# Attention pairs: rounded-half projections, modulation rows as VectorE dot products, turned values, and a softmax shared by two engines

## What is computed

```python
mod_x = silu(c) @ w_ada + b_ada            # 6 x 1024 values: shifts, scales, gates
ux = (rms_norm(x, norm1) * (1 + sc1) + sh1) @ w_in
uc = (rms_norm(xc, norm1) * (1 + csc1) + csh1) @ w_in
fx, qx, kx, vx, bx, cx, hx = split_in(ux)  # Fourier, q, k, v, conv parts
attn_x = na_latent(qx * scale, kx, vx, kc, vc, rpb)   # 8 heads of 64
x = x + g1 * mix_out(fx, attn_x, conv_x, w_fourier, w_out)
...                                        # then a hierarchical MoE of 32 experts,
...                                        # and four layers: sb, moba, swa, sb
```

## Time and profile before

| | |
|---|---|
| median of 3 runs | 2013.89 us (2011.30 to 2018.54) |
| profiled execution, its own time | 2015.65 us |
| its span | 2013.8 us, mean TensorE clock 0.972 |
| PE / PE weight loads / DVE / ACT / POOL busy | 1813.1 / 1450.8 / 1112.1 / 755.4 / 72.8 us |
| chain that ended last | PE 65%, DMA 24%, DVE 7%, ACT 2% |
| HBM read | 549.63 MB |

### The profile page before, as it was taken

How to read it: one execution, slowest core, us unless ns; L and a number is a source line. 1 busy time by engine, 2 the same in 40 slices (tenths; PEclk the granted TensorE clock), 3 DMA queues, 4 the chain that set the end, 5 groups by cost and what they waited for, 6 DMA issues and landing times.

```text
span 2013.8 us, 33860 instructions
## 1 busy us (share of the span) xinstructions
PE 1813.1 (90%) x14214; PEld 1450.8 (72%) x14214; DVE 1112.1 (55%) x1876; ACT 755.4 (38%) x1270; POOL 72.8 (4%) x131
## 2 busy tenths in 40 slices
PE   7999976776776789999999899999999999999998
PEld 5788744443443479788888688887688888988887
DVE  0233311101110278788677888764778877777774
ACT  2121200000000247644545654444554445755443
POOL 0200000000000000100000000000010000000000
PEclk8999999889899899999999999999999999999999
DMA  9457799999999975864773574466284578334533
GB/s 405 199 222 315 309 429 427 429 428 430 428 428 429 426 310 205 337 230 167 295 305 146 210 287 173 167 279 276 105 342 181 182 277 318 135 114 168 192 142 127
DMA packets 42186, 552.40 MB, mean 274 GB/s; under 512 B 6496, under 2 KB 6880, under 8 KB 7008
## 3 DMA queue, kind: packets, MB, share of 16 engines
q1 hardware_dynamic: 33408, 454.22, 56.7%
q0 software_dynamic: 8672, 96.67, 11.5%
HBM read 549.63 MB, written 1.05 MB: 273 GB/s over the span
## 4 chain that ended last, share of the span: by engine, by line
PE 65%; DMA 24%; DVE 7%; ACT 2%; issue 1%; SPq 0%; DVEq 0%; ACTq 0%
PE bank L594 24%; PE bank L595 12%; DMA ada_ring<-in_moe_side 12%; PE bank L589 10%; DMA ring<-in_moe 7%; PE bank L574 4%; PE bank L655 2%; DMA ring<-in_down 2%; PE bank L583 2%; PE bank L872 2%; PE bank L631 1%; DMA ring<-in_v 1%; DMA ring<-in_mix 1%; PE bank L1159 1%; PE bank L1027 1%
## 5 line engine op out<-in xcount | busy, mean ns | idle before, releaser
L595 PE MATMUL bank<-acts,ring_parts 128*128 128x256 f32 x2248 | 631.6, 281 | 0.0
L595 PEld LDWEIGHTS bank<-acts,ring_parts 128*128 128x128 f32 x2248 | 426.5, 190 | 0.0
L594 PE MATMUL bank<-acts,mixT_parts 128*128 128x512 f32 x1096 | 391.0, 399 | 6.3 <-DVE ring_parts L2395 6.0
L594 PE MATMUL bank<-acts,xn_parts 128*128 128x512 f32 x736 | 259.9, 396 | 0.0
L594 PEld LDWEIGHTS bank<-acts,mixT_parts 128*128 128x128 f32 x1096 | 207.1, 189 | 58.7 <-DVE ring_parts L2395 5.9
L1308 ACT CAST mixT_parts<-ring 128x1024 fp32r<-128x1024 f32 (+1 forms) x152 | 152.4, 1004 | 204.8 <-PE bank L595 184.9
L2059 DVE TENSOR_TENSOR mixT<-mixT,bank 128x128 f32<-128x128 f32 x32 | 9.2, 288 | 340.1 <-ACT mixT L1449 340.1
L594 PEld LDWEIGHTS bank<-acts,xn_parts 128*128 128x128 f32 x736 | 138.1, 188 | 32.9
L1308 ACT CAST xn_parts<-ring 128x1024 fp32r<-128x1024 f32 x96 | 100.2, 1052 | 141.2 <-PE bank L595 139.9
L589 PE MATMUL bank<-acts,ring_parts 128*128 128x256 f32 x504 | 141.7, 281 | 0.0
L2397 DVE TENSOR_TENSOR ring_parts<-ring,mixT_parts 128x1024 fp32r<-128x1024 f32 x88 | 107.7, 1225 | 30.0 <-ACT mixT_parts L1308 30.0
(11 more groups left out here) (326 smaller groups left out, 3166.4 us busy)
## 6 DMA issues: line engine op xcount, KB each, us to landing
ring<-in_moe SPq DMA_DIRECT2D x48, 2048.0 KB, 27.2
ada_ring<-in_moe_side SPq DMA_DIRECT2D x48, 2048.0 KB, 25.9
ada_ring<-in_ada POOLq DMA_DIRECT2D x45, 2048.0 KB, 13.4
ring<-in_gu SPq DMA_DIRECT2D x44, 2048.0 KB, 7.8
ring<-in_down SPq DMA_DIRECT2D x32, 1408.0 KB, 6.4
ring<-in_na SPq DMA_DIRECT2D x12, 2048.0 KB, 10.8
ring<-in_qk SPq DMA_DIRECT2D x12, 2048.0 KB, 9.4
ring<-in_out SPq DMA_DIRECT2D x10, 2048.0 KB, 9.0
```

The lines of the kernel that those rows point to most:

```text
L594: mm(dst[:, :], w[0], both(*x), start=start, stop=False)
L595: return mm(dst[:, 0:T], w[1], x[0], start=False, stop=stop)
```

## The change

- q, k, v weights of a pair come as three DMAs of 0.5 MB (`na_w`) into thirds of one slot; the two modulation chunks of a pair are laid out anew, one output column per partition.
- All projections of the pairs become `split_product`: `hT` and `hcT` are cut into halves once (`x_parts` in `xsq` and `hT`, `ctx_parts` in `ada_ring1`), and each third of the weights per pair (`cast_pair` on ACT, `low_pair` on DVE). v is projected like q and k (256 tokens moving), copied by ACT to `vt` and turned by four transposes on PE.
- The modulation rows are no longer PE's: DVE takes, per pair, eight dot products of 1024 elements per partition (`ada_dots`, `tensor_tensor_reduce`) against `c_row`, silu(c) repeated on all partitions, which PE makes once at the start from `c_spread` (two products of 512 columns, one DVE product ahead).
- Scores are laid out latent / context by bank; DVE scales and biases the latent half in two instructions of 128x512, ACT the context half; ACT also normalises (`ACT.Copy` with a scale per row) and copies all four banks of turned probabilities.
- The first pair's q, k and context k projections are placed between the steps of the Fourier section. The loops over pairs are unrolled.
- First sb layer: ACT's `group_out` moves from round j = 0 to round j = 1, behind the cast of `sp_hi`; PE's wait for it moves behind the scores of j = 1.

```diff
@@ SP @@
+                elif name == "na":
+                    for j in range(NA_PAIRS):
+                        def pair_weights(x, landed_in):
+                            if x == 2 or j == 0:
+                                wait_used(sp, n0 + 3 * j - RING)
+                            else:
+                                sp.wait_ge(na["qk_proj"] if x else na["q_used"], j)
+                            sp.dma_start(w_pair[x], ins["na_w"][3 * j + x]).then_inc(landed_in, 16)
...
+                        pair_weights(0, na["q_landed"])
+                        pair_weights(1, na["k_landed"])
+                        pair_mods(0)
+                        pair_weights(2, landed[n0 % RING])
+                        pair_mods(1)
@@ PE @@
+            def pair_project(dst, x, j, tokens, ready=None):
+                pe.wait_ge(attn_lo, 3 * j + x + 1)
+                lo = w_pair_lo[x].rearrange("p (k n) -> p k n", k=KT)
+                for k in range(KT):
...
+                    m = split_product(dst, (w_pair_hi[x][:, k, :], lo[:, k, :]), tuple(t[:, k, :] for t in tokens), k == 0, k == KT - 1)
+                return m
...
                 if not last:
-                    pe.wait_ge(na["qk_ready"], j + 1)
-                    ada(n0 + 1, bank[2][:, 0:T], r)
-                    ada(n0 + 2, bank[0][:, 0:T], r)
+                    pair_project(bank[1][:, T:2 * T], 2, j, ctx_parts).then_inc(used[n0 % RING], 1)
...
                 if not last:
-                    pe.wait_ge(na["ada_row"], j + 1)
-                    ada_columns(bank[2][:, 0:4], ada_rows[:, 0, :], 1)
-                    ada_columns(bank[2][:, 4:8], ada_rows[:, 1, :], 1).then_inc(na["ada_done"], 1)
+                    pe.wait_ge(na["vt_ready"], j + 1)
+                    for t in range(4):
+                        m = nc.tensor.transpose(bank[1][:, t * P:(t + 1) * P], vt[:, t * P:(t + 1) * P], cst("ident"))
+                    m.then_inc(na["row_done"], 1)
@@ ACT @@
             def na_pair(j, first, last):
+                if not first:
+                    act.wait_ge(na["scores"], j)
+                    for h in range(2):
+                        m = A(soft[:, 2 * h:2 * h + 2, T:2 * T], bank[6 + h][:, :].rearrange("p (q n) -> p q n", q=2), ACT.Copy, scale=SCALE)
+                    m.then_inc(na["s_ready"], 1)
+                if not first and not last:
+                    cast_pair(j, 2)
...
+                    act.wait_ge(na["step"], 2 * j)
+                    act.wait_ge(na["e_ready"], j)
+                    for c in range(4):
+                        m = A(prob[:, c, :], prob[:, c, :], ACT.Copy, scale=stat[:, 3, c:c + 1])
+                    m.then_inc(na["p_ready"], 1)
...
+                    wait_used(act, FIRST["na"], j)
+                    copy(vt, bank[1][:, :]).then_inc(na["vt_ready"], 1)
@@ DVE @@
+            def ada_dots(j, q0, q1):
+                for q in range(q0, q1):
...
+                    m = V.tensor_tensor_reduce(w, w, c_row, 1.0, 0.0, ALU.mult, ALU.add, stat[:, 4 + q // 4, q % 4:q % 4 + 1])
+                    if q % 4 == 3:
+                        m.then_inc(used[n % RING], 1)
@@ first sb layer, PE and ACT @@
+                            sb_scores(j)
                             if j == 1:
                                 pe.wait_ge(ada_taken, g + 1)
-                            sb_scores(j)
...
+                        if i == 0 and j == 1:
+                            group_out(group_of(i, 2), "attn")
                         if j < PAIRS - 1:
                             cast_piece(i, V_PIECES + 2 * (j + 1) + 1)
...
-                        if i == 0 and j == 0:
-                            group_out(group_of(i, 2), "attn")
```

More of the change, by code:

```diff
@@ L699, in _ @@
             m.then_inc(ada_cols, 1)
+            pe.wait_ge(na["row_ready"], 1)
+            for c in range(2):
+                m = mm(bank[6 + c][:, :], cst("ones"), c_spread[:, 512 * c:512 * (c + 1)], start=True, stop=True)
+            m.then_inc(na["row_done"], 1)
             n = FIRST["mix"]
             wait_chunk(pe, n)
-            rows(bank[0][:, :].rearrange("p (t n) -> p t n", t=TT), chunk3(n, 512), 0, T, hT, ready=0).then_inc(mix_proj, 1)
+            rows(bank[0][:, :].rearrange("p (t n) -> p t n", t=TT), chunk3(n, 512), 0, T, hT, ready=0).then_inc(mix_pe, 1)
             project(bank[1][:, 0:T], chunk3(n, 512), 256, hT)
@@ L792, in na_pair @@
                                 hp = slice(64 * h, 64 * h + 64)
[L793 removed]
+                                m = mm(bank[4 + 2 * a + h][:, q * T:(q + 1) * T], qk[hp, q * P:(q + 1) * P], keys[hp, :], start=True, stop=True)
                     m.then_inc(na["scores"], 1)
             na_pair(0, True, False)
[L797 removed]
+            for j in range(1, NA_PAIRS):
                 na_pair(j, False, False)
@@ L1420, in _ @@
             na_pair(0, True, False)
-            with act.Fori(1, NA_PAIRS) as j:
+            for j in range(1, NA_PAIRS):
                 na_pair(j, False, False)
@@ L1907, in na_pair @@
                     m.then_inc(na["s_ready"], 1)
-                    dve.wait_ge(na["s_ready"], j)
-                    V.tensor_reduce(stat[:, 0, :], soft[:, :, :], AX.X, ALU.max).then_inc(na["mx"], 1)
+                    dve.wait_ge(na["s_ready"], 2 * j)
+                    V.tensor_reduce(stat[:, 0, :], soft[:, :, :], AX.X, ALU.max).then_inc(na["step"], 1)
                     row_softmax_in(na, j)
+                if not last:
+                    low_pair(j, 2)
+                    ada_dots(j, 0, 2)
@@ L1938, in _ @@
             na_pair(0, True, False)
-            with dve.Fori(1, NA_PAIRS) as j:
+            for j in range(1, NA_PAIRS):
                 na_pair(j, False, False)
```

184 lines of the change are left out of this document (112 added, 72 removed).

## The result

The changed kernel takes **1985.45 us** (median of 4 runs, 1984.24 to 1988.75) against 2015.80 for the kernel before beside it (median of 4): ratio 0.986, 95% interval 0.9835 to 0.9885. It is faster by 1.4%; 1985 was forecast. The forecast took 28.7 us off a base of 2013.89, and the medians here stand 30.4 apart, so that the time itself came out within half a microsecond is partly luck. The profiled execution took 1985.69 us, its span is 1983.8, against 2015.65 and 2013.8.

A forecast was written before the change was run, and what follows sets the result against it. The prediction took PE to bound the pairs, busy 27.80 of 27.80 us. Its terms, -22.6 - 10.2 - 1.5 + 5.9 + 1.7 - 2.0 = -28.7, led from the median 2013.89 to 1985 us, range 1978 to 2007.

The forecast's parts named there:

- Dot products: DVE in the pairs: each 1024-element dot product with its sum costs 1.25 us, plus 0.1 for the read.
- Rival 1: DVE in the pairs: the dot runs at half rate, 2.3 us each, total 2005 us; chance 0.15.
- Rounds: Pairs after the first: 20.85 us, then 20.5 twice, 61.9 where 84.5 were; -22.6 us.
- DVE's loop without waits: DVE in a pair: 20.4 us, as long as PE's; also written 8c + 8.6, c the cost of a dot.
- First pair: From the Fourier section to the first scores: they end at 90.2 us instead of 100.4; -10.2 us.
- the clock term: PE at the start, 32 to 37 us: two products of 512 columns fill an idle stretch; -1.5 us.
- they delay nothing: Start of the kernel: the two 512-column products hold up nothing, since the first `mix` chunk lands behind them.
- out_0: Behind the last scores: output weights land 10.2 us after issue, so PE stands still 5.9 us; +5.9 us.
- clock +1.7: Output products: PE's wait for the output weights slows TensorE's clock after it; +1.7 us.
- sb layer: First sb layer: moving ACT's copy one round later removes PE's wait for q and k of j = 1; -2.0 us.
- Rival 3: Behind the pairs: the output weights are not late, -7.6 us more, total 1977 us; chance 0.09.
- rival 4: Expert stream: paced by transfers that can't start earlier, so the gain is absorbed, total 2011 us; chance 0.03.

The follow-up runs named there:

- doubled-dots kernel: Changed kernel with one extra 128x1024 DVE instruction ahead of each of the 32 dot products: 2012.12 us, ratio 0.9982.
- short dots: Changed kernel with dot products over 8 elements instead of 1024, so its modulation rows are wrong: 1986.48 us, ratio 0.9867.

## Why the prediction held

**Dot products.** 1.25 + 0.1 taken, 1.15 with its read measured, the lower bound. Rival 1 (half rate, 2.3 us) is out: the trace has 1.15. The Trainium skill's rule behind that rival (Vector Engine (DVE) Microarchitecture Reference, Points that are easy to get wrong) is that the scalar-tensor-tensor layout with two non-bf16 SBUF sources halves throughput. It doesn't price this dot, which the trace shows as CUSTOM_DVE_ANT_0; whether that operation has the layout no row says. A row of before that the prediction did not show bears on the rule too, a scalar-tensor-tensor with both f32 tensors in SBUF, without a sum:

```profile
L1977 DVE SCALAR_TENSOR_TENSOR ada_ring<-ada_ring,c_wide 128x512 f32<-128x512 f32 x96 | 66.5, 746 | 0.0
```

It takes 746 ns for 512 columns, where a plain two-source row of that size (L2413) has 685: not halved. Had rival 1's price held, the doubled-dots kernel shows what the change would have brought: a few us, not 30.

**Rounds.** 20.85 + 20.5 + 20.5 = 61.9 forecast, 3 x 20.63 = 61.89 measured. The total is right, and its closeness is luck: PE's own round was put at 20.4 and is 20.63 (four projections 11.66 for 11.5, turned v 0.59 for 0.44), and the 0.65 us that was added over the three rounds for DVE's lateness made up for it. DVE was 1.06 us late behind the first pair (its scaling starts at 90.24, the scores end at 89.18), not 1.8, and that delayed no round of PE. The sentence that DVE's loop without waits is 20.4 was wrong by its own steps: they add to about 18.6 at 1.25 us a dot, and 8c + 8.6 gives 18.6 too; measured, DVE is busy 18.24 us in a round of 20.63. So PE was the bound by more than the prediction thought.

**First pair and clock.** Forecast first scores -10.2 and -1.5, measured -11.26 together. In this profile the clock term was half its size: the fall of the clock went, but the c_row products delay the mixing products by 0.96 us (33.41 against 32.45), because the head chunk ahead of them was taken up at 27.78 instead of 26.93. Here the step "they delay nothing" did not hold. It depends on when that chunk lands: the second profile has 27.16 and a delay of 0.35, and the kernels with doubled and with short dots start the mixing products at 32.43 and 32.46, without a delay, and end the transform near 67.2. But then PE does wait for DVE's remainders in q and k, as the prediction foretold, and the first scores end at 88.5 to 88.7 all the same. So the two terms together are -11.3 to -11.9, where -11.7 was forecast. The first pair itself took 21.0 us from the end of the transform, 21.3 forecast. In this profile its q and k end at 73.95 without the foretold wait for DVE.

**out_0.** +5.9 forecast, and 5.9 measured less the 0.24 that before had too; clock +1.7, measured +1.57 (2.75 in the second profile, 15.07 against 12.32). These four add up to -26.6 at the end of the output products, which is where both traces stand apart by 26.64.

**What was not in the sum**: another dip of the clock in the routing (0.91 from 200 to 220 us: L683 takes 2.89 us instead of 1.86, L889 4.33 instead of 3.73), which costs 1.6. It comes and goes: the kernels with `out_0` one half at a time and with short dots have 1.00 there, with the same work, and the kernel before with the sb move alone has such a dip (0.91 from 220 to 240 us), so it isn't the change's.

**sb layer.** -2.0 forecast, 1.9 measured, and 1.9 with this edit alone.

At the fourth head pair the traces stand 28.1 apart; the sum said 28.7. That nearness is again partly luck: the 1.6 us of the routing dip are outside the sum, and 1.2 of them came back in the experts, where profiles of one kernel differ by more. Behind that layer the lead falls to 26.5 (one dip of the clock in the changed kernel, L683 3.49 us instead of 1.86), rises to 28.3 over a wait for a chunk of `in_down`, 13.18 us where the profile of before has 14.95, and to 29.8 behind it, where the clock of before averages 0.95 over 36 us and that of the changed kernel 1.00. No edit touches these places; the dip at L683 is not in the second profile. Rival 3 (out_0 not late) and rival 4 (gain absorbed) did not occur: the expert stream moved by 25.0 and was no shorter in its waits of 27.3 us. In one reason the prediction was too simple: it took `out_0`'s 10.2 us as twice 5.1, halved by POOL. The two runs without that share give 7.6 and 9.1.

## What to carry to other kernels

When one engine is busy 100% of a loop and another a third, moving small matrix-vector work (here 4.6 us of PE per round) to the idle one is free until its loop is as long; write both loops as a sum with the unknown price in it, and you have the break-even before you have the price. Before shortening a stage, ask which transfer is issued in its last steps: its time doesn't shrink with the stage. Here another order of two chunks, together with POOL's later one, was worth about 8 us more in the traces and 11 in the medians. It needed no faster transfer, only a slot that was free earlier, so that the first chunk was issued at 140.2 instead of 146.7.

## What the runs showed of the hardware

- The dot product with a sum (CUSTOM_DVE_ANT_0 in the trace) runs at the rate of a subtraction: 1.15 us for 128x1024 f32, read of the sum included.
- A single 2 MB transfer with nothing behind it in its queue landed after 9.12 us, though its bytes moved at up to 442 GB/s; with the next chunk queued behind it 7.60; beside POOL's equal chunk 10.04 to 11.86 in ten profiles. That it lands later alone than with the next chunk behind it no trace here explains.
- The fall of TensorE's clock to its lower level (1.2 of 2.4 GHz) cost 1.6 to 2.8 us over the 56 output products (13.89 to 15.07 instead of 12.3), whether PE had stood for 2.1, 3.3 or 5.9 us: a wait of 2 us can cost nearly as much again.
